# Delta net in a two-block model: the triangle built transposed, beta on its columns, and the transposed inverse taken by VectorE's transpose

## The chip, the cores and the metric

The kernel runs on one core of one Trainium2 chip. A core has TensorE (matrix products into PSUM), VectorE, ScalarE, GpSimd and SyncE (here it issues the loads of the weights), and 16 DMA engines. Times are device microseconds (us) of the whole program; the median of several executions counts.

## What is computed

Two transformer blocks on 256 tokens of width 1024, all in float32. The first block mixes the tokens in four groups of four heads (attention with forget gates, "fox"; gated delta net, "gdn"; and two gated linear attentions), the second by a short convolution and by differential attention; each ends in gated feed-forward layers. The change lies in the delta net of the first block alone. Cut to what matters:

```python
def gated_delta_chunked(q, k, v, g, beta):      # 4 heads, 4 chunks of 64 tokens, dk = dv = 64
    G = cumsum(g) within a chunk
    decay = exp(where(causal, G[r] - G[s], -inf))
    kb = k * beta[r]
    m = where(strict, (kb[r] . k[s]) * decay, 0)
    t_mat = m + I
    w = solve(t_mat, kb * exp(G)[r])
    u = solve(t_mat, v * beta[r])
    a_qk = where(causal, (q[r] . k[s]) * decay, 0)
    q_in, k_out = q * exp(G)[r], k * exp(G[-1] - G)[r]
    # over the chunks, one after the other:
    v_new = u - w @ state
    o = q_in @ state + a_qk @ v_new
    state = state * exp(G[-1]) + k_out.T @ v_new
```

The solves are done as products with the inverse of `t_mat`, a unit triangle of 64 by 64 for each of 16 pairs of head and chunk.

## The kernel before

**Weights.** All products with weights take them in blocks of 1 MB (a block is `[128, 2048]` float32), in a ring of three slots. SyncE loads block n into `raw` (`weights_in`, L462; blocks 12 and 13 in four pieces, one waiting for the other, L469 and L472) once the low part of block n-3 has been made. ScalarE rounds it to `w_hi` (`block_hi`, L1511), VectorE makes the rest `w_lo = raw - w_hi` (`block_lo`, L2263; halves of it by `half_lo`, L2693), and TensorE does three products for each pair of operands: hi x hi, lo x hi, hi x lo. `quarter(n, q)` is one fourth of block n, 12 products of 128x256; `project(n, f)` is half a block, 24 products. TensorE's instructions stand in the order in which the functions are called; so do those of the other engines. Semaphores alone tie them together.

**The delta net.** Partitions hold the 128 tokens of two chunks; a "unit" u of 8 is a pair of chunks of one head. The calls of TensorE in order, with what is written beside them by the others:

- `gdn_grams`: in PSUM bank 2 the logarithms of the decays (products with constant masks), in banks 0 and 1 the gram k.k, in banks 6 and 7 the gram k.q. ScalarE takes the exponential into `dec` (L1729).
- `gdn_turn_decay`: 16 products of 64x64 with the identity turn `dec`; ScalarE copies the result into `dec_t` (L1734, two copies of 64x512). Meanwhile VectorE makes `m_gd` = gram x beta x dec, eight instructions (L2445).
- `gdn_turn_m`, after `project(7, 1)`: 16 more such products turn `m_gd`, and ScalarE copies them into `mt_gd` (L1734 again).
- VectorE makes the first approximations of the inverse in blocks of 32x32, exact in blocks of two: `inv` from `m_gd` (`gdn_first_inverse`, L2460 to L2464) and its transpose `inv_t` from `mt_gd` (`gdn_first_turned`, L2468 to L2476), with `a_qk` = gram k.q x dec_t between them (L2453).
- Five levels follow, TensorE's loop below. In each, `gdn_cx` (16 products with 64 rows and 32 columns) multiplies `c_t`, the part of `mt_gd` that belongs to the level (VectorE, L2481), by `inv`; ScalarE copies it to `y_gd` (L1748). `gdn_xcx` then forms inv x y twice in levels 0 to 3: once as it is (bank 6) and once transposed (bank 0), 32 products of 32x32 each, and VectorE subtracts the one from `inv` and the other from `inv_t` (L2488, two instructions). Level 4 has 32 products of 32x32 only, and joins the two halves of a chunk in `inv_full`.
- `gdn_solve` multiplies `inv_full` by `vb` (v x beta) and `kbg` (k x beta x exp G), and four chunks follow.

```python
            project(7, 0)
            gdn_grams()
            gdn_turn_decay()
            project(7, 1)
            gdn_turn_m()
            project(8, 0)
            fills = [(8, 2), (8, 3), (9, 0), (9, 1), ...
            for lv in range(5):
                gdn_cx(lv)
                quarter(*fills[2 * lv])
                gdn_xcx(lv)
                quarter(*fills[2 * lv + 1])
            gdn_solve()
```

VectorE's order there is: `block_lo(7)`, `block_lo(8)`, `gdn_grams`, `gdn_first_inverse`, `gdn_first_turned`, `block_lo(9)`, and then for each level the next `c_t` (`gdn_next_block`), other work (`fox_sums` after level 0, the two halves of block 10 in levels 1 and 2, `fox_scale` in level 3, `gla_queries_and_keys` and `block_lo(11)` in level 4), and `gdn_xcx`. ScalarE's order: the exponential, the copies of the turned decays, `tokens_from(fox_v)` (L1648, results of block 7), the copies of the turned m, `block_hi(9)`, and the levels.

Lines: every product goes through one of two helpers, so that L538 (`mm`) and L587 (`add`) are lines of many places. A small float32 product shows as two records in the trace: 16 products are 32 rows.

Of the kernel before, what the change touches and what calls it, by code (L numbers as in the profile page):

```python
# [91 lines left out]
def low_base(f):  # L92
# [11 lines left out]
    "decay_by_act": ("decay", "decay_t", "mt_ready"),  # L104
    "grams": ("decay_logs", "qk_gram", "decay_turned", "m_turned"),
# [16 lines left out]
def build(nc, weights, small_in, x_in, masks_in, ident_in, channel_in, row_in, w_gk_in, p_in, table_in,  # L122
# [4 lines left out]
    with ExitStack() as ctx:  # L127
# [33 lines left out]
        gd_hi = sb("gd_hi", [P, TT, HEADS], R)  # L161
        gd_lo = sb("gd_lo", [P, TT, HEADS], R)
# [43 lines left out]
        be_g = place([P, TT, HEADS])  # L206
# [9 lines left out]
        kbg = place([P, 8, DH])  # L216
        vb = place([P, 8, DH])
# [8 lines left out]
        dec = place([P, 8, CHUNK])  # L226
        m_gd = place([P, 8, CHUNK])
# [3 lines left out]
        ngd_tri = place([P, 8, CHUNK])  # L231
        HALF = CHUNK // 2
        two_blocks = lambda v: [b.rearrange("p u n -> p (u n)").rearrange("p (u n) -> p u n", n=HALF) for b in (v[:, 0:4, :], v[:, 4:8, :])]
        inv, inv_t = two_blocks(dec)
        y_gd, pair_t_odd = two_blocks(m_gd)
# [86 lines left out]
        def block_mask(name):  # L322

            at = MASK["blocks0"] * P + ("eye", "pair_even", "pair_odd", "pair_t_even", "pair_t_odd").index(name) * HALF
            return masks.rearrange("p m n -> p (m n)")[:, at:at + HALF]
# [210 lines left out]
        def _(pe):  # L536
# [423 lines left out]
            def gdn_grams():  # L960
# [3 lines left out]
                for part in (gd_hi, gd_lo):  # L964
# [7 lines left out]
                add(o, mask("same"), ngd_tri.rearrange("p u n -> p (u n)"), False, True).then_inc(once("decay_logs")[0], 1)  # L972
# [14 lines left out]
            def gdn_turn_decay():  # L987
                pe.wait_ge(*once("decay"))
                turn_chunks(2, dec).then_inc(once("decay_turned")[0], 1)

            def gdn_turn_m():
                pe.wait_ge(sem("m_ready"), 1)
                turn_chunks(0, m_gd).then_inc(once("m_turned")[0], 1)
# [31 lines left out]
            def gdn_solve():  # L1025
                pe.wait_ge(sem("inv_t_ready"), 6)
                for t, h in ALL_UNITS:
                    m, u = u_of(t, h), t * HEADS + h
                    for c in range(2):
                        r = rows_of_chunk(c)  # L1030
                        mm(chunk_bank(2, u, c), inv_full[r, m, :], vb[r, u, :])
                for t, h in ALL_UNITS:
# [3 lines left out]
                    for c in range(2):  # L1036
                        r = rows_of_chunk(c)
                        last = mm(PS[a:a + 64, c, at:at + CHUNK], kbg[r, u, :], inv_full[r, m, :])
# [203 lines left out]
            gdn_turn_decay()  # L1242
            project(7, 1)
            gdn_turn_m()
# [249 lines left out]
        def _(act):  # L1494
# [240 lines left out]

            def gdn_turn_decay():
                act.wait_ge(*once("decay_turned"))
                chunk_copy(dec_t, 2, 0)
                chunk_copy(dec_t, 2, 1).then_inc(once("decay_t")[0], 1)

            def gdn_turn_m():
                act.wait_ge(*once("m_turned"))
                chunk_copy(mt_gd, 0, 0)
                chunk_copy(mt_gd, 0, 1).then_inc(once("mt_ready")[0], 1)
# [121 lines left out]
            gdn_turn_decay()  # L1866
            tokens_from(BLOCK_OF["fox_v"])
            gdn_turn_m()
# [370 lines left out]
        def _(dve):  # L2239
# [119 lines left out]
            def gate_parts():  # L2359
# [3 lines left out]
                mark(dve.tensor_copy(gd_hi[:, :, :], gd))  # L2363
                settle()
                mark(tt(nlf_lo[:, :, :], nlf, nlf_hi[:, :, :].bitcast(F), ALU.subtract))
                mark(tt(gd_lo[:, :, :], gd, gd_hi[:, :, :].bitcast(F), ALU.subtract))
# [15 lines left out]
            def gate_products():  # L2382
                dve.wait_ge(*once("gate_exps"))
                mark(tt(be_g, beta, e_g, ALU.mult))
# [1072 lines left out]
```

## Time and profile before

| | us |
|---|---|
| median of 3 executions | 1026.76 (1026.28 to 1027.33) |
| the profiled execution | 1027.2 |
| its span in the profile | 1025.4 |
| TensorE busy in the span | 1004.7 (98%) |
| VectorE busy | 845.2 (82%) |
| ScalarE busy | 621.6 (61%) |
| DMA, mean over the span | 172 GB/s |
| mean granted clock of TensorE | 0.997 of full speed |

The delta net's triangle and inverse take the stretch from about 56 to 96 us of the span. A row of the chain gives a start, a duration and the work; a row of the timeline merges instructions of one form that follow one another, and a bracket at its end tells how long the engine had been idle, and what ended that. PE is TensorE, DVE VectorE, ACT ScalarE, SPq SyncE's queue.

### The profile page before, as it was taken

How to read it: one execution, taken by the hardware profiler on the slowest of the kernel's cores; microseconds unless marked ns; L12 is line 12 of the kernel's file. 1: busy time of each engine (PE TensorE's matmuls, PEld its weight loads, DVE VectorE, ACT ScalarE, POOL GpSimd, SP SyncE). 2: the span in 40 equal slices, each digit the busy share in tenths (PEclk: the TensorE clock that was granted, in tenths of full speed). 3: DMA queues.
4: the chain of work that ended last, by engine and by line, in shares of the span. 5: the costliest groups of instructions: out<-in, count | busy, mean ns of one | idle time of the engine just before them, and what ended most of it. 6: DMA issues, size and time to landing. Idle time of an engine off the chain costs nothing.

```text
span 1025.4 us, 21307 instructions
## 1 busy us (share of the span) xinstructions
PE 1004.7 (98%) x8589; PEld 940.3 (92%) x8589; DVE 845.2 (82%) x1211; ACT 621.6 (61%) x856; POOL 5.8 (1%) x16
## 2 busy tenths in 40 slices
PE   6999999999999999999999999999999999999996
PEld 6998899999999999899999999999999999999985
DVE  5974797699988878878999888799775899988876
ACT  6763565566665655556665555676676666565665
POOL 0000000000000000000000000000000000000000
PEclk9999999999999999999999999999999999999998
DMA  8533223455655544566566555444534356555531
GB/s 322 180 110 106 87 81 126 161 179 204 205 197 177 199 165 165 178 234 217 185 209 208 197 194 175 154 176 151 179 124 148 126 200 205 206 196 179 198 124 42
DMA packets 26500, 176.02 MB, mean 172 GB/s; under 512 B 3229, under 2 KB 3509, under 8 KB 6080
## 3 DMA queue, kind: packets, MB, share of 16 engines
q1 hardware_dynamic: 25616, 171.31, 48.5%
q0 software_dynamic: 816, 3.73, 1.2%
q8 instruction: 52, 0.85, 0.3%
q14 instruction: 16, 0.13, 0.0%
HBM read 173.97 MB, written 2.63 MB: 172 GB/s over the span
## 4 chain that ended last, share of the span: by engine, by line
PE 92%; DVE 4%; ACT 3%; issue 1%; DMA 0%; SPq 0%; DVEq 0%; ACTq 0%
PE PS L587 79%; PE PS L538 12%; DVE w_lo L2263 1%; ACT w_hi L1511 1%; DMA raw<-weights 0%; PE PS L1416 0%; DVE arena L2660 0%; DVE h_store L2276 0%; PE PS L807 0%; PE PS L777 0%; ACT arena L1831 0%; ACT arena L1625 0%; DVE x L2780 0%; DVE arena L2915 0%; PE PS L939 0%
## 5 line engine op out<-in xcount | busy, mean ns | idle before, releaser
L587 PE MATMUL PS<-h_store,w_hi 128*128 128x256 f32 (+1 forms) x1840 | 483.4, 340 | 9.2 <-DVE w_lo L2315 8.0
L2263 DVE TENSOR_TENSOR w_lo<-raw,w_hi 128x2048 fp32r<-128x2048 f32 x156 | 357.0, 2290 | 54.8 <-ACT w_hi L1511 49.6
L587 PE MATMUL PS<-h_store,w_lo 128*128 128x256 f32 (+1 forms) x1400 | 373.2, 282 | 0.6 <-issue 0.6
L587 PEld LDWEIGHTS PS<-h_store,w_hi 128*128 128x128 f32 x1840 | 308.2, 188 | 50.1 <-DVE w_lo L2315 8.0
L1511 ACT ACTIVATE w_hi<-raw 128x2048 fp32r<-128x2048 f32 x156 | 297.9, 1910 | 76.3 <-PE PS L587 66.3
L587 PEld LDWEIGHTS PS<-h_store,w_lo 128*128 128x128 f32 (+1 forms) x1400 | 257.2, 189 | 1.0 <-issue 0.8
L587 PE MATMUL PS<-act_hi,w_hi 128*128 128x256 f32 x704 | 196.2, 280 | 0.2 <-DVE act_hi L2870 0.2
L587 PE MATMUL PS<-act_hi,w_lo 128*128 128x256 f32 x704 | 195.1, 279 | 0.0
L587 PE MATMUL PS<-act_lo,w_hi 128*128 128x256 f32 x704 | 192.0, 279 | 0.0
L587 PEld LDWEIGHTS PS<-act_hi,w_hi 128*128 128x128 f32 x704 | 132.4, 188 | 2.9 <-issue 1.3
L587 PEld LDWEIGHTS PS<-act_hi,w_lo 128*128 128x128 f32 x704 | 132.3, 188 | 0.0
L587 PEld LDWEIGHTS PS<-act_lo,w_hi 128*128 128x128 f32 x704 | 130.4, 188 | 0.0
L1946 ACT ACTIVATE arena<-PS 128x512 f32<-128x512 f32 x51 | 30.2, 592 | 87.2 <-PE PS L587 87.2
L1938 ACT ACTIVATE arena<-arena,channel 128x256 f32<-128x256 f32 x132 | 63.7, 531 | 22.4 <-DVE arena L2964 15.6
L587 PE MATMUL PS<-w_hi,h_store 128*128 128x256 f32 (+1 forms) x352 | 71.4, 307 | 0.0
L2941 DVE SCALAR_TENSOR_TENSOR arena<-arena,channel 128x254 f32<-128x254 f32 x132 | 57.9, 480 | 7.6 <-DVE arena L2937 0.3
L2937 DVE SCALAR_TENSOR_TENSOR arena<-arena,channel 128x255 f32<-128x255 f32 x132 | 57.7, 478 | 3.8 <-ACT arena L1938 3.8
L587 PEld LDWEIGHTS PS<-w_hi,h_store 128*128 128x128 f32 x352 | 54.4, 188 | 3.5 <-issue 0.4
L2962 DVE TENSOR_TENSOR arena<-PS,arena 128x512 f32<-128x512 f32 x51 | 34.9, 685 | 20.6 <-ACT arena L1946 20.6
L587 PE MATMUL PS<-w_lo,h_store 128*128 128x256 f32 (+1 forms) x176 | 45.8, 302 | 0.0
L538 PE MATMUL PS<-arena 32*32 32x32 f32 (+7 forms) x1548 | 44.9, 222 | 0.9 <-DVE arena L2660 0.4
L538 PE MATMUL PS<-h_store,w_hi 128*128 128x256 f32 x256 | 45.4, 279 | 0.0
(365 smaller groups left out, 1103.0 us busy)
## 6 DMA issues: line engine op xcount, KB each, us to landing
raw<-weights SPq DMA_DIRECT2D x155, 1024.0 KB, 4.9
raw<-weights SPq DMA_DIRECT2D x12, 256.0 KB, 3.5
arena<-masks_in SPq DMA_DIRECT2D x1, 1600.0 KB, 11.6
bias_by_key<-bias_by_distance POOLq DMA_DIRECT2D x1, 1536.0 KB, 8.7
x<-x_in SPq DMA_DIRECT2D x4, 256.0 KB, 4.6
raw<-weights SPq DMA_DIRECT2D x2, 512.0 KB, 8.4
arena<-bias_by_key POOLq DMA_DIRECT2D x1, 1024.0 KB, 7.2
result<-arena SPq DMA_DIRECT2D x4, 256.0 KB, 2.1
```

Of the source, the lines that this page charges most:

```text
L538: return pe.matmul(o, lhs, rhs, start=start, stop=stop)
L587: return pe.matmul(o, lhs, rhs, start=start, stop=stop, skip_group_check=True)
L1511: act.activation(w_hi[:, slot, :], raw[:, slot, :], ACT.Copy).then_inc(hi_ready, 1)
L1938: ins = act.activation(dst[:, c, :], src[:, c, :], ACT.Identity, scale=w, bias=b)
L1946: act.activation(low, PS[:, bank:bank + 2, TOK:512], ACT.Copy).then_inc(sem("low_copied"), 1)
L2263: tt(w_lo[:, slot, :], raw[:, slot, :], w_hi[:, slot, :].bitcast(F), ALU.subtract).then_inc(lo_ready, 1)
L2937: stt(y[:, c, 1:TOK], src[:, c, 0:TOK - 1], channel[:, bass.ds(col(1) + c, 1)], y[:, c, 1:TOK], ALU.mult, ALU.add).then_inc(ready[0], 1)
L2941: ins = stt(y[:, c, 2:TOK], src[:, c, 0:TOK - 2], channel[:, bass.ds(col(0) + c, 1)], y[:, c, 2:TOK], ALU.mult, ALU.add)
L2962: tt(z, PS[:, bank:bank + 2, 0:TOK], low, ALU.add).then_inc(sem("parts_added"), 1)
```

## The change

The triangle is built transposed at once. The constant mask and the sign of the decays' operands are exchanged (`ngd` for `gd`), so that bank 2 holds the logarithms of the transposed decays, and the exponential goes straight to `dec_t`. The gram k.k is symmetric, so gram x beta x dec_t is a transposed triangle, `mt_gd`, with beta on the other index than before. That is another triangle, M' with beta on its columns, and the identity between the two moves beta: v and k go to the solve without it (`v_gd`, `kg`), and it comes back in `ko` (through `be_rest` = beta x e_rest) and in `a_qk`, which is now eight instructions as `mt_gd` is. `gdn_turn_decay` and `gdn_turn_m` are gone on TensorE and on ScalarE. VectorE makes `inv_t` from `mt_gd` and takes `inv` by a transpose of 32x32 blocks; in levels 0 to 3 TensorE forms the product once, VectorE subtracts it from `inv` and transposes the result into `inv_t`. Core of the diff:

```diff
@@ PE @@
                 add(o.rearrange("p (u n) -> p u n", n=CHUNK), exact("eye"), units(exact("gdn_add")[:, 0:CHUNK], 8), start=True)
-                for part in (gd_hi, gd_lo):
+                for part in (ngd_hi, ngd_lo):
...
-            def turn_chunks(bank, v):
-
-                for u in range(8):
-                    for c in range(2):
-                        r = rows_of_chunk(c)
-                        last = mm(chunk_bank(bank, u, c), v[r, u, :], ident[r, r])
-                return last
...
                 if lv < 4:
-                    block_products(6, inv_t, y_gd).then_inc(sem("xcx"), 1)
-                    block_products(0, y_gd, inv_t).then_inc(sem("xcx"), 1)
+                    block_products(0, inv_t, y_gd).then_inc(sem("xcx"), 1)
                     return
...
             gdn_grams()
-            gdn_turn_decay()
             project(7, 1)
-            gdn_turn_m()
             project(8, 0)
@@ ACT @@
-                act.activation(flat(dec), PS[:, 2, :], ACT.Exp).then_inc(once("decay")[0], 1)
+                act.activation(flat(dec_t), PS[:, 2, :], ACT.Exp).then_inc(once("decay")[0], 1)
...
             gdn_grams()
-            gdn_turn_decay()
             tokens_from(BLOCK_OF["fox_v"])
-            gdn_turn_m()
             block_hi(9)
@@ DVE @@
-                mark(tt(vb, psu(2), unit(th(beta), DH), ALU.mult))
+                mark(dve.tensor_copy(v_gd, psu(2)))
...
-                mark(tt(kbg, kn, unit(th(be_g), DH), ALU.mult))
-                mark(tt(ko, kn, unit(th(e_rest), DH), ALU.mult))
+                mark(tt(kg, kn, unit(th(e_g), DH), ALU.mult))
+                mark(tt(ko, kn, unit(th(be_rest), DH), ALU.mult))
...
             def gdn_a_qk():
-                dve.wait_ge(*once("decay_t"))
+
                 dve.wait_ge(*once("qk_gram"))
-                by_bank = lambda v: v.rearrange("p (b u) n -> p b (u n)", b=2)
-                tt(by_bank(a_qk), PS[:, 6:8, 0:256], by_bank(dec_t), ALU.mult).then_inc(sem("qk_gram_read"), 1)
+                for t, h in ALL_UNITS:
+                    u = u_of(t, h)
+                    mark(stt(a_qk[:, u, :], PS[:, 6 + u // 4, (u % 4) * CHUNK:(u % 4 + 1) * CHUNK], beta[:, t, h:h + 1], dec_t[:, u, :],
+                             ALU.mult, ALU.mult))
+                settle()
 
             def gdn_first_inverse():
 
-
-                dve.wait_ge(sem("m_ready"), 1)
-                dve.wait_ge(*once("decay_turned"))
-                mark(tt(inv, m_gd[:, :, 0:HALF], units(block_mask("pair_even"), 8), ALU.mult))
-                mark(tt(inv_t, m_gd[:, :, HALF:CHUNK], units(block_mask("pair_odd"), 8), ALU.mult))
-                settle()
-                link(tt(inv, units(block_mask("eye"), 8), inv, ALU.subtract))
-                tt(inv, inv, inv_t, ALU.subtract).then_inc(sem("inv_ready"), 1)
-
-            def gdn_first_turned():
-                dve.wait_ge(*once("mt_ready"))
-                tt(c_t, mt_gd, units(packed(1), 8), ALU.mult).then_inc(sem("ct_ready"), 1)
-                gdn_a_qk()
-                dve.wait_ge(sem("qk_gram_read"), 1)
-                dve.wait_ge(sem("inv_ready"), 1)
                 mark(tt(inv_t, mt_gd[:, :, 0:HALF], units(block_mask("pair_t_even"), 8), ALU.mult))
                 mark(tt(pair_t_odd, mt_gd[:, :, HALF:CHUNK], units(block_mask("pair_t_odd"), 8), ALU.mult))
                 settle()
+                tt(c_t, mt_gd, units(packed(1), 8), ALU.mult).then_inc(sem("ct_ready"), 1)
                 link(tt(inv_t, units(block_mask("eye"), 8), inv_t, ALU.subtract))
                 tt(inv_t, inv_t, pair_t_odd, ALU.subtract).then_inc(sem("inv_t_ready"), 1)
+                dve.wait_ge(sem("inv_t_ready"), 1)
+                dve.transpose(inv, inv_t).then_inc(sem("inv_ready"), 1)
...
                 if lv < 4:
-                    for k, (x_gd, ready) in enumerate(((inv, sem("inv_ready")), (inv_t, sem("inv_t_ready")))):
-                        dve.wait_ge(sem("xcx"), 2 * lv + k + 1)
-                        tt(flat(x_gd), flat(x_gd), PS[:, 6 - 6 * k, 0:8 * HALF], ALU.subtract).then_inc(ready, 1)
+                    dve.wait_ge(sem("xcx"), lv + 1)
+                    tt(flat(inv), flat(inv), PS[:, 0, 0:8 * HALF], ALU.subtract).then_inc(sem("inv_ready"), 1)
+                    dve.wait_ge(sem("inv_ready"), lv + 2)
+                    dve.transpose(flat(inv_t), flat(inv)).then_inc(sem("inv_t_ready"), 1)
                     return
...
             gdn_grams()
             gdn_first_inverse()
-            gdn_first_turned()
+            gdn_a_qk()
             block_lo(9)
```

What TensorE has in a row around the two turns, as a piece of the difference (a count is of products, each two records of the trace; 64x64 rows on the identity are the turns; 128x256 rows belong to blocks 7 and 8):

```order
 L538 MATMUL PS<-arena 64x64 x16
 L587 MATMUL PS<-arena 128x512
 L538 MATMUL PS<-arena 64x64 x16
-L538 MATMUL PS<-ident,arena 64x64 x16
 L587 MATMUL PS<-w_hi,h_store 128x256 x16
 L587 MATMUL PS<-w_lo,h_store 128x256 x8
-L538 MATMUL PS<-ident,arena 64x64 x16
 L587 MATMUL PS<-w_hi,h_store 128x256
```

Two groups of 16 products left the queue, and the 24 products of `project(7, 1)` now follow the grams at once. In levels 0 to 3 the same engine has, each time:

```order
-L538 MATMUL PS<-arena 32x32 x64
+L538 MATMUL PS<-arena 32x32 x32
```

Half of the products of 32x32 are gone. VectorE's row from `block_lo(7)` and `block_lo(8)` to the product of level 0, before (L2445 is m_gd, L2460 to L2464 the first `inv`, L2468 `c_t`, L2453 `a_qk`, L2472 to L2476 `inv_t`, L2263 `block_lo`, L2481 the next `c_t`, L2488 the subtractions of `gdn_xcx`):

```order
59 L2263 TENSOR_TENSOR w_lo<-raw,w_hi 128x2048 x2
60 L2445 SCALAR_TENSOR_TENSOR arena<-PS,arena 128x64 x8
61 L2460 TENSOR_TENSOR arena<-arena 128x256
62 L2461 TENSOR_TENSOR arena<-arena 128x256
63 L2463 TENSOR_TENSOR arena<-arena 128x256
64 L2464 TENSOR_TENSOR arena<-arena 128x256
65 L2468 TENSOR_TENSOR arena<-arena 128x512
66 L2453 TENSOR_TENSOR arena<-PS,arena 128x512
67 L2472 TENSOR_TENSOR arena<-arena 128x256
71 L2263 TENSOR_TENSOR w_lo<-raw,w_hi 128x2048
72 L2481 TENSOR_TENSOR arena<-arena 128x512
73 L2488 TENSOR_TENSOR arena<-arena,PS 128x256 x2
```

And of the changed kernel (L2415 is `mt_gd`, L2430 and L2431 the masked pairs, L2433 `c_t`, L2434 and L2435 the subtractions, L2424 `a_qk`, L2232 `block_lo`, L2442 the next `c_t`, L2448 the one subtraction of `gdn_xcx`):

```order
60 L2415 SCALAR_TENSOR_TENSOR arena<-PS,arena 128x64 x8
61 L2430 TENSOR_TENSOR arena<-arena 128x256
62 L2431 TENSOR_TENSOR arena<-arena 128x256
63 L2433 TENSOR_TENSOR arena<-arena 128x512
64 L2434 TENSOR_TENSOR arena<-arena 128x256
65 L2435 TENSOR_TENSOR arena<-arena 128x256
66 L2437 STREAM_TRANSPOSE arena<-arena 128x256
67 L2424 SCALAR_TENSOR_TENSOR arena<-PS,arena 128x64 x8
68 L2232 TENSOR_TENSOR w_lo<-raw,w_hi 128x2048
69 L2442 TENSOR_TENSOR arena<-arena 128x512
70 L2448 TENSOR_TENSOR arena<-arena,PS 128x256
71 L2450 STREAM_TRANSPOSE arena<-arena 128x256
```

One row of first approximations is left of two, `a_qk` stands behind it and is eight instructions, and a transpose stands at the end of it and behind each level's subtraction.

## Rows read from the trace of the kernel before

**Rows 1.** The page, busy time, share of the span and instructions by engine.

```profile
PE 1004.7 (98%) x8589; PEld 940.3 (92%) x8589; DVE 845.2 (82%) x1211; ACT 621.6 (61%) x856; POOL 5.8 (1%) x16
```

**Rows 2.** Waits of TensorE over the span: us in total, times, longest.

```profile
PE PS L587 <- DVE w_lo L2315: 8.0, 1, 8.0
...
PE PS L587 <- issue: 0.6, 1, 0.6
...
PE PS L538 <- DVE arena L2660: 0.4, 1, 0.4
```

**Rows 3.** The chain that ended last, 57 to 96 us: start, us, work, records.

```profile
58.55 1.84 PE PS L538 x61
60.39 3.03 PE PS L587 x24
63.42 1.08 PE PS L538 x32
64.50 3.04 PE PS L587 x24
67.53 1.05 PE PS L538 x32
68.58 1.61 PE PS L587 x12
70.19 1.16 PE PS L538 x78
71.35 0.07 issue
71.42 0.27 PE PS L538 x9
...
75.96 1.24 PE PS L538 x83
...
83.48 0.57 issue
...
93.35 0.68 PE PS L538 x50
94.03 1.61 PE PS L587 x12
```

**Rows 4.** Timeline of VectorE, 57 to 96 us.

```profile
59.22 1.62 DVE L2445 SCALAR_TENSOR_TENSOR arena<-PS,arena 128x64 f32<-128x64 f32 x8 [0.72 <-ACT arena L1729]
60.88 0.43 DVE L2460 TENSOR_TENSOR arena<-arena 128x256 f32<-128x256 f32 x1
...
65.78 0.69 DVE L2468 TENSOR_TENSOR arena<-arena 128x512 f32<-128x512 f32 x1 [3.22 <-ACT arena L1734]
...
68.70 2.28 DVE L2263 TENSOR_TENSOR w_lo<-raw,w_hi 128x2048 fp32r<-128x2048 f32 x1
...
72.17 1.21 DVE L2584 TENSOR_REDUCE stat<-arena 128x16 f32<-128x1024 f32 x1
...
75.02 1.22 DVE L2693 TENSOR_TENSOR w_lo<-raw,w_hi 128x1024 fp32r<-128x1024 f32 x1
...
92.32 0.34 DVE L2491 TENSOR_SCALAR arena<-arena 128x256 f32<-128x256 f32 x1
94.08 0.48 DVE L2493 TENSOR_SCALAR arena<-PS,arena 128x256 f32<-128x256 f32 x1 [1.42 <-PE PS L538]
```

**Rows 5.** Timeline of ScalarE, 57 to 96 us.

```profile
60.43 1.20 ACT L1734 ACTIVATE arena<-PS 64x512 f32<-64x512 f32 x2 [1.25 <-PE PS L538]
63.46 0.84 ACT L1648 ACTIVATE arena<-PS,xn 128x256 f32<-128x256 f32 x2 [1.83 <-PE PS L587]
...
65.77 1.92 ACT L1511 ACTIVATE w_hi<-raw 128x2048 fp32r<-128x2048 f32 x1
```

**Rows 6.** Timeline of SyncE's queue, 57 to 96 us: block 12.

```profile
71.01 6.89 SPq L469 DMA_DIRECT2D raw<-weights  x3
80.77 0.31 SPq L472 DMA_DIRECT2D raw<-weights  x1
```

More of the change, by code:

```diff
@@ L103 @@
     "fox_by_dve": ("fox_sums", "fox_normed"),
-    "decay_by_act": ("decay", "decay_t", "mt_ready"),
-    "grams": ("decay_logs", "qk_gram", "decay_turned", "m_turned"),
+    "decay_by_act": ("decay",),
+    "grams": ("decay_logs", "qk_gram"),
     "bias_by_act": ("bias_rows", "lambda_exps"),
@@ L160, in build @@
         nlf_lo = sb("nlf_lo", [P, TT, HEADS], R)
-        gd_hi = sb("gd_hi", [P, TT, HEADS], R)
-        gd_lo = sb("gd_lo", [P, TT, HEADS], R)
+        ngd_hi = sb("ngd_hi", [P, TT, HEADS], R)
+        ngd_lo = sb("ngd_lo", [P, TT, HEADS], R)
         zeros_r = sb("zeros_r", [P, 512], R)
@@ L205, in build @@
         e_last = place([P, TT, 2, 2])
-        be_g = place([P, TT, HEADS])
+        be_rest = place([P, TT, HEADS])
         sq = place([P, 1024])
@@ L215, in build @@
         kn = place([P, 8, DH])
-        kbg = place([P, 8, DH])
-        vb = place([P, 8, DH])
+        kg = place([P, 8, DH])
+        v_gd = place([P, 8, DH])
         ko = place([P, 8, DH])
@@ L225, in build @@
         a_qk = place([P, 8, CHUNK])
-        dec = place([P, 8, CHUNK])
-        m_gd = place([P, 8, CHUNK])
+        inverses = place([P, 8, CHUNK])
+        y_and_pairs = place([P, 8, CHUNK])
         dec_at = arena["at"]
@@ L230, in build @@
         c_t = place([P, 8, CHUNK])
-        ngd_tri = place([P, 8, CHUNK])
+        gd_tri = place([P, 8, CHUNK])
         HALF = CHUNK // 2
         two_blocks = lambda v: [b.rearrange("p u n -> p (u n)").rearrange("p (u n) -> p u n", n=HALF) for b in (v[:, 0:4, :], v[:, 4:8, :])]
-        inv, inv_t = two_blocks(dec)
-        y_gd, pair_t_odd = two_blocks(m_gd)
+        inv, inv_t = two_blocks(inverses)
+        y_gd, pair_t_odd = two_blocks(y_and_pairs)
         inv_full = dec_t
@@ L971, in gdn_grams @@
                         mm(gram_bank(0, t, h, c), k, k)
-                add(o, mask("same"), ngd_tri.rearrange("p u n -> p (u n)"), False, True).then_inc(once("decay_logs")[0], 1)
+                add(o, mask("same"), gd_tri.rearrange("p u n -> p (u n)"), False, True).then_inc(once("decay_logs")[0], 1)
                 for c in range(2):
@@ L1030, in gdn_solve @@
                         r = rows_of_chunk(c)
-                        mm(chunk_bank(2, u, c), inv_full[r, m, :], vb[r, u, :])
+                        mm(chunk_bank(2, u, c), inv_full[r, m, :], v_gd[r, u, :])
                 for t, h in ALL_UNITS:
@@ L1037, in gdn_solve @@
                         r = rows_of_chunk(c)
-                        last = mm(PS[a:a + 64, c, at:at + CHUNK], kbg[r, u, :], inv_full[r, m, :])
+                        last = mm(PS[a:a + 64, c, at:at + CHUNK], kg[r, u, :], inv_full[r, m, :])
                 last.then_inc(sem("solved"), 1)
@@ L2362, in gate_parts @@
                 mark(dve.tensor_copy(nlf_hi[:, :, :], nlf))
-                mark(dve.tensor_copy(gd_hi[:, :, :], gd))
+                mark(dve.tensor_copy(ngd_hi[:, :, :], ngd))
                 settle()
                 mark(tt(nlf_lo[:, :, :], nlf, nlf_hi[:, :, :].bitcast(F), ALU.subtract))
-                mark(tt(gd_lo[:, :, :], gd, gd_hi[:, :, :].bitcast(F), ALU.subtract))
+                mark(tt(ngd_lo[:, :, :], ngd, ngd_hi[:, :, :].bitcast(F), ALU.subtract))
                 settle()
@@ L2383, in gate_products @@
                 dve.wait_ge(*once("gate_exps"))
-                mark(tt(be_g, beta, e_g, ALU.mult))
+                mark(tt(be_rest, beta, e_rest, ALU.mult))
                 signal(sem("gk_read"), 1)
@@ L3404, in mask_table @@
     i_blk, j_blk = r % 32, c[:, 0:32]
-    pair = (i_blk // 2 == j_blk // 2) & (j_blk < i_blk)
     pair_t = (i_blk // 2 == j_blk // 2) & (i_blk < j_blk)
-    blocks = [i_blk == j_blk, pair & (i_in < 32), pair & (i_in >= 32), pair_t & (i_in < 32), pair_t & (i_in >= 32)]
-    blocks += 3 * [i_blk < 0 * j_blk]
+    blocks = [i_blk == j_blk, pair_t & (i_in < 32), pair_t & (i_in >= 32)]
+    blocks += 5 * [i_blk < 0 * j_blk]
     for j in range(4):
@@ L3419, in mask_table @@
     one["fox_add"] = np.where(c <= r, 0.0, NEG)
-    one["gdn_add"] = np.concatenate([np.where(j_in <= i_in, 0.0, NEG), i_in <= j_in], axis=1)
+    one["gdn_add"] = np.concatenate([np.where(i_in <= j_in, 0.0, NEG), i_in <= j_in], axis=1)
     rows = [one[n] + np.zeros((P, P)) for n in MASKS]
```

28 lines of the change are left out of this document (7 added, 21 removed).

## The prediction

> **What bounds the kernel now.** I read the busy times first [rows 1]: TensorE is busy 98% of the span. The waits of TensorE come next [rows 2], to see whether the missing 2% hide a chain of other engines: apart from 8.0 us for the first weights there is one wait of 0.6 us that the profile puts down to issue, and small ones of 0.2 to 0.4 us in later places. So TensorE's queue is what sets the end, and an instruction taken out of it is worth its full time, as long as its operands come early enough for the earlier start. Third, the chain inside the delta net [rows 3]: from 58.55 us on it is nothing but TensorE, group behind group, with two pieces of issue. In this view each group of products has its own price, and those are the prices that I add up. VectorE and ScalarE idle there: VectorE waited 3.22 us for ScalarE's copy of the turned m [rows 4], ScalarE 1.25 and 1.83 us for TensorE [rows 5].
>
> **What TensorE loses.** The second turn is the group of 32 records at 63.42 us, 1.08 us. The first stands in one piece with the gram k.q, 61 records in 1.84 us; at the price of the second it takes 1.08 of them and leaves 0.76 to the gram [rows 3]. Both are gone: 2.16 us.
>
> In levels 0 to 3 the group of 64 products of 32x32 (128 records, of which the chain names some) becomes one of 32. Level 4 already has a group of 32 such products, and it took 0.68 us [rows 3]. That is the price I take for each of the four. A whole group took 1.24 us in level 1, and levels 2 and 3 repeat it: 3 x (1.24 - 0.68) = 1.68 us. Level 0 took 1.16 + 0.07 + 0.27 = 1.50 us, with an issue gap late in the group [rows 3]; 1.50 - 0.68 = 0.82 us. I count that gap as gone, since the group now ends before the place in it where the gap was. Had it stayed, the sum would be 0.26 us smaller. Sum: 2.16 + 1.68 + 0.82 = 4.66 us, some 4.7.
>
> The 0.57 us of issue at 83.48 us [rows 3] lies in a run of plain 128-wide products behind level 2. Nothing that the profile shows was awaited, and I leave it in the sum. If it is TensorE running out of fetched instructions after dense groups of tiny products, it may go, since 192 records leave in front of it in levels 0 to 2 and 64 in the turns; that is a rival below.
>
> The Trainium skill bears on this: "Runtime: NRT & Kernel Launch", section Instruction fetch mechanics, says that the sequencer fetches its instructions in blocks of 16 KiB while it executes, mostly hidden, and that branches are what breaks it. By that rule a straight piece of code would have no such gap; the trace has one of 0.57 us in straight code.
>
> **What the new order asks of VectorE.** With the turns out, TensorE is done with the grams at 58.55 + 0.76 = 59.31 us, with `project(7, 1)` 3.03 us later, 62.34, and with `project(8, 0)` at 65.38, where the products of level 0 want `inv` and `c_t` (before: 67.53) [rows 3]. VectorE's side: the eight instructions on the gram end at 59.22 + 1.62 = 60.84 as before, since the exponential comes at the same time. Two masked products of 0.43 each (overlapping a little), to 61.7; `c_t`, 0.69, to 62.4; two dependent subtractions of 0.43, to 63.2; then the transpose [rows 4]. No transpose of VectorE is in this trace. It handles 128x256 elements in one instruction, as the rows of 0.34 (one operand, SBUF) and 0.48 (PSUM) do; 0.43 us of the two-operand row lies between them, and I take that. From below it can't be under the 0.34 of the plain row by much; from above I take the longest row of VectorE there, 2.28 us [rows 4]. At 0.43 `inv` is ready at 63.7, with 1.7 us to spare; even at 2.28 the wait would be 0.2 us. So the wait that is added costs nothing up to a transpose of 2.1 us.
>
> A page has a price for it: the Trainium skill, "VectorE: DVE Perf Modes", section The three transpose paths, gives 311 ns for a 128x128 transpose in bf16 by VectorE and 390 ns by TensorE. No run here shows that figure. Scaled by columns it makes 0.4 to 0.6 us for 256 columns (an estimate from that page), and the sum would stay the same.
>
> Behind the transpose: `a_qk`, now eight instructions, 1.62 us for 0.7, and `block_lo(9)`, 2.28 us. From 63.7 they end at 65.3 and 67.6, if ScalarE has block 9 rounded. ScalarE loses four copies (1.20 us for each two), takes the results of block 7 from 62.4 on, 0.84 us, and rounds block 9 in 1.92 us, to 65.3 [rows 5]: just in time. Who waits behind `block_lo(9)`: the next `c_t`, ready at 68.3, wanted by level 1 at 70.3; TensorE for block 9, wanted at 71.4; and SyncE for block 12, whose load in four pieces (from 71.01 us on, the last issued at 80.77) now starts at 67.6 and so lands some 3 us earlier [rows 6], still before ScalarE's turn for it in level 3. So none is late.
>
> In a level TensorE now takes 1.05 + 1.61 + 0.68 + 1.61 = 4.95 us [rows 3]. After the product VectorE subtracts (0.48 at most, PSUM source), and `inv` is ready 1.1 us before the next level starts; this was so before. The transpose comes behind it, and `inv_t` is wanted only 1.61 + 1.05 + 1.61 us after the product's end. In a level VectorE gives up one subtraction for one transpose, no change. At the end the last wait, VectorE's joining of the halves (0.48) under one quarter of a block (1.61), is as before [rows 4]. The copy of v instead of a multiplication, and the moved beta, have the shapes of what they replace, far ahead of TensorE's need; costed at nothing, cover being the grams and `project(7, 0)`.
>
> So the stretch ends 4.7 us earlier, and the later stages, with TensorE as full as here, carry it to the end. The sum stands against the profiled execution, span 1025.4 in 1027.2: span 1020.7, execution 1022.5. That execution is 0.4 above the median of 1026.76, so the median comes to **1022.1 us**.
>
> **The rivals.**
> - *The issue gap goes too.* For: it stands in the densest part of TensorE's code, and is the only one over the whole span of that length on the engine; 256 records leave ahead of it. Against: it lies 0.8 us behind the small products, among plain ones. It gives 1022.1 - 0.6 = 1021.5. Only chance decides where it falls, so 37%.
> - *Fewer products, but not shorter groups.* In `gdn_cx` 32 records take 1.05 us [rows 3], more than the 64 records of level 4: the count isn't the whole price. If a group in which each product writes `PS` with a new weight costs 1.05 us here, a level saves 0.2 us, and all 2.16 + 3 x 0.19 + 0.45 = 3.2 us: 1023.6. Against it stands level 4 with the same shapes at 0.68. 8%.
> - *The transpose turns into the wait.* From 2.1 us on, `inv` is late for level 0. In the levels VectorE has, between the product of level 0 and that of level 4, four subtractions (1.9), the sums of squares (1.2), three `c_t` (2.1), two halves of block 10 (2.4), `fox_scale` (about 1.4 by the row of 1024 elements and one small one), the queries and `block_lo(11)` (3.1): 12 us and four transposes, in 4 x 4.95 = 19.8 us of TensorE. So four transposes bind from 2.0 to 2.2 us each, and each us more costs 1 + 4 = 5 us. Between 2.2 and 3.1 us the gain shrinks to nothing; that is the case of a time near 1025, 6%.
> - *Slower than before.* The same mechanism from 3.1 us a transpose on, seven times the row of 0.43: the five transposes then hold VectorE, and TensorE waits in every level. At 4 us it gives 5 x (4 - 3.1) = 4.5 us more than before, 1031. It would take a rate that no instruction of VectorE shows here. 3%.
>
> **How the numbers follow.** Forecast 44%, gap gone 37%, short saving 8%, transpose partly in the way 6%, slower 3%, 2% for others. From the first two and the third the range is 1021.5 - 0.5 to 1023.6 + 0.5, the half being the spread of the shown runs about their median: 1021.0 to 1024.1, which leaves out about 15%. A measurement tells about 0.2% (2 us) from no change: faster needs a time under 1024.7. All of the first three cases are, and half of the transposes' case: 0.91. Same 0.05, slower 0.04.
>
> **What will show it.** In the chain of the changed kernel `project(7, 1)` should start at 59.3 and level 0 at 65.4, the groups in levels 0 to 3 be 64 records in 0.68 us, and the solve start near 91 us (before 95.6). The transposes should be rows of 0.3 to 0.6 us on VectorE. TensorE's waits should show none on VectorE in that stretch; one in front of the products with `c_t` would say that the transpose or the chain to it is late. If the solve starts 4.7 us earlier and the end doesn't, a later stage is bound by something else than TensorE, which these rows deny.

## The result, and the profile after

The changed kernel takes 1021.01 us (median of 5 executions, 1020.74 to 1021.24), the one before 1026.51 in the same measurement (5 executions, 1026.28 to 1027.33); ratio 0.9944, 95% interval 0.9931 to 0.9958. It is faster by 5.5 us. The forecast was 1022.1 with a range from 1021.0: the way was right, the gain was underrated by 0.8 us (4.7 forecast, 5.5 measured), and the time stands on the very edge of the range. The profiled execution has a span of 1019.0 us (1025.4 before).

The chain of the changed kernel in the delta net, 57 to 92 us (start, us, work, records); it answers to [rows 3]:

```profile
57.66 0.91 PE PS L538 x30
58.57 5.87 PE PS L587 x48
64.44 1.05 PE PS L538 x32
65.49 1.61 PE PS L587 x12
67.11 0.68 PE PS L538 x50
67.79 1.62 PE PS L587 x12
...
77.01 0.68 PE PS L538 x50
77.69 1.61 PE PS L587 x12
79.30 1.05 PE PS L538 x32
...
89.24 1.60 PE PS L538 x62
```

The two turns are gone, so that 48 records of the projections stand in one piece; each group of 32x32 products takes 0.68 us; and the quarter at 77.69, the one behind level 2, takes 1.61 us without an issue gap. Set against the starts of before this gives the account. "Lead" is how much earlier the same work starts in this trace:

| | before | after | lead |
|---|---|---|---|
| second set of grams (k.q) | 58.55 | 57.66 | 0.89 |
| products with `c_t`, level 0 | 67.53 | 64.44 | 3.09 |
| quarter behind level 0's products | 71.68 | 67.79 | 3.89 |
| quarter behind level 2's products | 82.71 | 77.69 | 5.02 |
| products with `c_t`, level 3 | 85.15 | 79.30 | 5.85 |
| the solve | 95.65 | 89.24 | 6.41 |
| end of the span | 1025.4 | 1019.0 | 6.4 |

The turns gave 2.20 us (forecast 2.16), level 0 gave 0.80 (0.82), levels 1 and 2 together 1.13 (1.12), level 3 the remaining 0.56. That is 4.7 us, the forecast's sum. The quarter behind level 2 gave another 0.83: that is the issue gap, gone. The 0.89 us of lead at the grams lies ahead of the part that lost instructions. Over the fourteen traces of this study the first set of grams starts anywhere between 54.85 and 56.81 us, whatever the kernel, so it is spread between executions. Without it this pair of traces has 4.7 + 0.8 = 5.5 us, which is also the distance of the medians. But the interval of the ratio allows 4.3 to 7.1 us, so that the medians alone can't tell 4.7 from 5.5; the traces do.

VectorE in the same stretch (timeline, start and us first), answering to [rows 4]:

```profile
58.33 1.63 DVE L2415 SCALAR_TENSOR_TENSOR arena<-PS,arena 128x64 f32<-128x64 f32 x8 [0.70 <-ACT arena L1710]
...
62.31 0.45 DVE L2437 STREAM_TRANSPOSE arena<-arena 128x256 f32<-128x256 f32 x1
62.68 1.58 DVE L2424 SCALAR_TENSOR_TENSOR arena<-PS,arena 128x64 f32<-128x64 f32 x8
64.39 2.29 DVE L2232 TENSOR_TENSOR w_lo<-raw,w_hi 128x2048 fp32r<-128x2048 f32 x1
```

The transpose takes 0.45 us (0.43 taken) and ends at 62.76, 1.7 us before level 0 wants it (1.7 forecast). TensorE's waits show none on VectorE in this stretch.

### The profile page after: what moved, and what is told of

It reads as the page before. It is cut to its first block, busy times and chain, and to the rows that moved or that the text cites. A ratio compares the mean times of both kernels' runs of the same rounds, so it can differ in the third digit from the quotient of the medians.

```text
span 1019.0 us, 20665 instructions
## 1 busy us (share of the span) xinstructions
PE 998.6 (98%) x8269; PEld 934.9 (92%) x8269; DVE 845.2 (83%) x1215; ACT 619.2 (61%) x852; POOL 5.8 (1%) x16
## 4 chain that ended last, share of the span: by engine, by line
PE 92%; DVE 4%; ACT 3%; issue 1%; DMA 0%; SPq 0%; DVEq 0%; ACTq 0%
PE PS L587 79%; PE PS L538 12%; DVE w_lo L2232 1%; ACT w_hi L1492 1%; DMA raw<-weights 0%; PE PS L1397 0%; DVE arena L2622 0%; DVE h_store L2245 0%; PE PS L807 0%; PE PS L777 0%; ACT arena L1802 0%; ACT arena L1606 0%; DVE x L2742 0%; DVE arena L2877 0%; DVE arena L2771 0%
## 5 line engine op out<-in xcount | busy, mean ns | idle before, releaser
L2232 DVE TENSOR_TENSOR w_lo<-raw,w_hi 128x2048 fp32r<-128x2048 f32 x156 | 357.1, 2290 | 54.7 <-ACT w_hi L1492 49.4
L538 PE MATMUL PS<-arena 64*64 64x64 f32 (+7 forms) x1292 | 42.3, 227 | 0.9 <-DVE arena L2622 0.4
```

The source lines that it names most:

```text
L538: return pe.matmul(o, lhs, rhs, start=start, stop=stop)
L2232: tt(w_lo[:, slot, :], raw[:, slot, :], w_hi[:, slot, :].bitcast(F), ALU.subtract).then_inc(lo_ready, 1)
```

## The experiments

Two things were open. Where did the gap of 0.83 us go, and was its going luck? And is VectorE's slack as large as the sum said, that is, would a slower transpose have turned the change into a loss at the point named? Theory P: the gap sits at fixed places of TensorE's instruction stream, where the next piece of code has not yet come, and it comes with a dense stream of tiny products. Rivals: an accident of one execution (C), or something that follows dense work after a time, wherever that lies (D). The texts below that were put on record before the runs say F for the first form of P: TensorE runs out of fetched instructions behind dense groups of tiny products.

**The kernel before once more.** No edit.

> The kernel before, unchanged, for a second look at its trace. Theory F (the gap is TensorE running out of fetched instructions behind dense groups of tiny products): an issue gap of about 0.8 us of weight loading stands again in the same quarter of level 2, since the instructions lie at the same places. Theory C (the gap is an accident of one execution): it is missing or elsewhere. The first 56 us: in the first trace the grams began at 56.6 us, in the changed kernel's at 55.7; if that is spread of single executions, the grams start here anywhere from 55.7 to 56.6.

1026.44 us in its one execution. Its chain, in level 0 and in and behind level 2:

```profile
69.90 1.26 PE PS L538 x87
...
80.94 1.24 PE PS L538 x83
82.18 0.78 PE PS L587 x5
82.96 0.27 issue
```

The gap stands at the same instruction, smaller (0.27 us; the weight loads stood still for 0.47, for 0.78 in the first trace), and the quarter takes 2.14 us instead of 1.61, so that here it costs 0.53. The gap of level 0 isn't there at all: its group takes 1.26 us in one piece, 1.50 in the first trace. The grams start at 56.3 us, with no change of code: the start spreads. The weight loads (PEld) of the first trace, beside this:

```profile
70.12 1.14 PEld L538 LDWEIGHTS PS<-arena 32*32 32x32 f32 x120
71.42 0.15 PEld L538 LDWEIGHTS PS<-arena 32*32 32x32 f32 x8 [0.16 <-issue]
...
84.06 0.19 PEld L587 LDWEIGHTS PS<-h_store,w_lo 128*128 128x128 f32 x1 [0.78 <-issue]
```

The two gaps lie behind record 120 of level 0 and behind record 5 of the quarter behind level 2. By the calls that is 8 + 12 + 32 + 12 + 128 + 12 + 32 + 12 + 128 + 5 = 381 records.

**The second set of products put back**, result unused:

```diff
                 if lv < 4:
+                    block_products(1, y_gd, inv_t)
                     block_products(0, inv_t, y_gd).then_inc(sem("xcx"), 1)
```

> The changed kernel with the second set of 32 products of 32x32 put back in levels 0 to 3, its result unused. Sum of the prediction: 4 x 0.56 us of products, so 1021.0 + 2.3 = 1023.3. Theory F adds the gap where density brings it back: 1023.3 + 0.8 to 1.1 = 1024.3. Theory C: 1023.3, no gap in the levels.

1025.9 us (10 executions, 1024.14 to 1028.11), ratio to the kernel before 0.9995, 0.9985 to 1.0004. Half of the products that had been taken away cost nearly the whole gain. Chain of its profiled execution, and TensorE's windows (stretch, its length, busy, granted clock, DMA share and GB/s):

```profile
67.51 1.22 PE PS L538 x82
...
73.00 1.20 PE PS L538 x81
74.19 1.78 issue
75.97 0.24 PE PS L538 x2
76.21 1.68 PE PS L587 x12
77.90 1.85 PE PS L538 x32
79.75 2.86 PE PS L587 x12
82.61 1.86 PE PS L538 x128
```

```profile
74.00:76.00 2.00, 0.22 (x23) 1.00 0.51 131
76.00:78.00 2.00, 2.00 (x18) 0.90 0.35 70
78.00:80.00 2.00, 2.00 (x33) 0.50 0.21 70
```

An ordinary group takes 1.22 us (1.24 in the kernel before), so products are worth 4 x 0.54. But in level 1 a gap of 1.78 us opens two records before the end of the group, and some 1.6 us behind it the granted clock falls from 1.00 to 0.50, TensorE's lower level of 1.2 GHz. The same groups then take 1.85 instead of 1.05, 2.86 instead of 1.61 and 1.86 instead of 1.22 us. TensorE had stood for 1.8 us of otherwise unbroken work before the clock fell.

This trace is of the slowest of the ten executions, 1028.11 us. Three of them (1027.15 to 1028.11) have a mean granted clock of 0.995, the other seven (1024.14 to 1026.17, median 1025.7) 0.998, as the kernel before has; so the drop of the clock is a thing of three in ten. The seven are still 2.5 us above the 1023.2 of the products alone. A gap of the size seen here would be 1.8 of them; no trace of such an execution was kept, so that is not shown.

**The turns put back**, results unused (the two groups of 16 products stand where they stood before; ScalarE copies nothing):

```diff
             gdn_grams()
+            pe.wait_ge(*once("decay"))
+            turn_chunks(2, dec_t)
             project(7, 1)
+            pe.wait_ge(sem("ct_ready"), 1)
+            turn_chunks(0, mt_gd)
             project(8, 0)
```

> The changed kernel with the 32 products of 64x64 of the two turns put back at their places, their results unused (ScalarE doesn't copy them). The chains of before and after put the turns at 2.2 us: 1021.0 + 2.2 = 1023.2. Both theories of the gap expect none here, since the levels keep their 32 products.

1022.33 us (5 executions, 1021.74 to 1023.19), ratio 0.9963, 0.9949 to 0.9977. From the start of the first grams to the solve its chain takes 90.56 - 54.85 = 35.71 us, the changed kernel's 89.24 - 55.70 = 33.54: the turns cost 2.17 us, and no gap came. The medians differ by 1.3 us only (2.2 forecast); the start of an execution spreads by 2 us, which is enough to hide the rest, but that it did is not shown.

**Both put back.**

> Both put back: TensorE has as many instructions as before, with the new work of VectorE and ScalarE. Theory F: everything is back on TensorE, gap included: 1026.5, as before. Theory C: 1021.0 + 2.2 + 2.3 = 1025.5 with no gap.

1026.65 us (10 executions, 1026.09 to 1028.62), ratio 1.0004, 0.9994 to 1.0013: as before the change. So VectorE's and ScalarE's side of the change is worth nothing by itself; all of it is TensorE's. Its chain has the gap in the same quarter as before:

```profile
80.97 1.22 PE PS L538 x82
82.18 0.78 PE PS L587 x5
82.96 0.73 issue
83.69 1.09 PE PS L587 x7
```

Five records into the quarter behind level 2, as in [rows 3] and in the second trace of the kernel before. With the products put back and the turns away, the code in front was 64 records shorter and the gap came in level 1 instead. Accident (C) falls. Between D and P the next three decide: they move the code in the stream, and nothing else.

**The kernel before, with 16 or 32 tiny products in front**, in TensorE's idle first 8 us:

```diff
+            pe.wait_ge(*once("ones_set"))
+            for _ in range(16):        # 32 in the second
+                mm(PS[0:32, 3, 0:32], ones_r[0:32, 0:32].bitcast(F), ones_r[0:32, 0:32].bitcast(F))
             first_columns()
```

> The kernel before with 16 tiny products (32x32 on ones, result unused, 32 records) put in front of everything, in TensorE's idle first 8 us. They cost no time by themselves. Theory P (the gap sits at a fixed place of TensorE's instruction stream, a boundary at which the next piece of code has not come yet): the gap moves 32 records earlier, from the fifth group of the quarter behind level 2 into the products of level 2, near record 101 of 128. Theory D (it comes a certain time behind dense work, wherever that lies): it stays in the quarter behind level 2.

1027.47 us in its one execution. Weight loads (PEld), timeline of level 2:

```profile
81.56 0.97 PEld L538 LDWEIGHTS PS<-arena 32*32 32x32 f32 x101
83.24 0.33 PEld L538 LDWEIGHTS PS<-arena 32*32 32x32 f32 x27 [0.72 <-issue]
```

The gap moved from record 128 + 5 to record 101: by 32 records, as P said to the record. The execution has a smaller gap too, which costs 0.21 us in the products with `c_t` of level 2 (1.26 us for 1.05): the weight loads pause behind the 17th of 32, which is 15 + 12 + 101 = 128 records ahead of the large one.

> The same with 32 tiny products (64 records) in front. Theory P: the gap stands near record 69 of the 128 of level 2. Theory D: as in the trace of before, in the quarter behind level 2. For the time: 1026.5 plus or minus 1 by both, more if the gap grows beyond a us and takes the clock down as in the kernel with the products put back.

1026.69 us in its one execution. Here the place was missed: nothing near record 69 of level 2, but a gap in level 1 and one behind level 3:

```profile
74.08 1.18 PEld L538 LDWEIGHTS PS<-arena 32*32 32x32 f32 x126
...
90.01 1.01 PEld L538 LDWEIGHTS PS<-arena 64*64 64x64 f32 x32 [1.32 <-issue]
```

Counted by the calls, the two places are 382 records apart. The gap of level 1 (two records before the end of the group) and the place forecast in level 2 (record 69) are 127 apart: 2 + 12 + 32 + 12 + 69. So there are boundaries every 127 to 128 records (each comes with a weight load, so some 256 instructions), and at which of them TensorE has to stand is not fixed by the place alone; the speed at which it came there is the other part, as the dense and the thin versions show. P holds in that form. The two gaps of the trace with the products put back and with both put back are 255 records apart in the stream, which is twice that. The page's row of the instructions' own queue (packets, MB, share) fits; for the changed kernel it is

```profile
q8 instruction: 49, 0.80, 0.3%
```

16.3 KB a packet. With the turns put back (64 records and as many weight loads, 128 instructions) it counts 50, with the products (512 instructions) 51, with both, as in the kernel before (640), 52: with 256 instructions a packet these are 0.5, 2 and 2.5 packets more, where only whole ones count. The 52 don't hold the whole code, since TensorE's records and weight loads alone are 17,178; the row can be trusted for differences here, not for the total. The Trainium skill, "Runtime: NRT & Kernel Launch", section Instruction fetch mechanics, names blocks of 16 KiB or 256 instructions; the traces agree. It calls crossing one mostly hidden and finds the trouble in branches; here straight code shows gaps up to 1.8 us, so in dense streams of tiny products the measurement decides against it.

The kept traces show the arrival itself. Each packet of that queue is in them with its time. The last one before the end of each gap (us from the start of the span):

| trace | last code packet, start and duration | TensorE goes on | behind the packet's end |
|---|---|---|---|
| before, level 0 | 68.73, 1.33 | 71.42 | 1.36 |
| before, behind level 2 | 81.74, 0.94 | 84.06 | 1.38 |
| before once more | 80.64, 1.29 | 83.23 | 1.30 |
| products put back | 73.08, 1.32 | 75.97 | 1.57 |
| both put back | 81.09, 1.17 | 83.69 | 1.43 |
| before, 16 in front | 80.67, 1.22 | 83.25 | 1.36 |
| before, 32 in front, level 1 | 73.65, 0.96 | 75.98 | 1.37 |
| before, 32 in front, behind level 3 | 87.12, 1.05 | 89.80 | 1.63 |

In all eight gaps TensorE goes on 1.3 to 1.6 us behind the end of a packet of code, while the packets come 3.5 to 9 us apart there. That is what a wait for code looks like, and neither C nor D would tie the end of a gap to a packet. What decides when a packet starts isn't shown: at one and the same boundary the gap was 0.27, 0.57 and 0.73 us long in three executions. The loads of weights use the same 16 DMA engines and are a possible cause that no run separates.

**The products put back, with 32 tiny products in front**, so that the levels stand where they stood before the change:

> The changed kernel with the second set of products put back in the levels, and 32 tiny products in front, so that the levels stand at the same places of TensorE's stream as in the kernel before (the turns were 64 records). Theory P: the gap of 1.8 us in level 1 and the drop of the clock behind it are gone, and a gap of 0.5 to 0.9 us stands in the quarter behind level 2, as before: 1021.0 + 2.3 + 0.8 = 1024.1, against 1025.9 without the shift. Theory D: as without the shift, 1025.9.

1024.76 us (10 executions, 1023.20 to 1025.97), ratio 0.9983, 0.9973 to 0.9992, against 1025.9 without the shift. Its chain:

```profile
77.94 1.22 PE PS L538 x82
79.16 0.78 PE PS L587 x5
79.94 0.97 issue
80.92 1.09 PE PS L587 x7
```

The gap is back in the quarter behind level 2, the one of 1.78 us is gone, and in this trace the clock stays at 1.00 throughout the levels. In both gaps of this trace TensorE again goes on 1.3 to 1.4 us behind the end of a code packet. By the medians the kernel with 64 records more, which compute nothing, is 1.1 us faster; the intervals of the two ratios (0.9973 to 0.9992, 0.9985 to 1.0004) overlap a little, so the place of the gap in the trace carries the argument more than the time. D says neither.

**The transpose, four and eight times over.**

```diff
+                for _ in range(3):        # 7 in the second
+                    link(dve.transpose(inv, inv_t))
                 dve.transpose(inv, inv_t).then_inc(sem("inv_ready"), 1)
```

and likewise in the levels.

> The changed kernel with each transpose of VectorE done four times over (the same result), so that it takes 4 x 0.46 = 1.85 us. The prediction's slack says that up to 2.0 to 2.1 us nothing waits: 1021.0, the solve as early as before. If instead the transpose was on the edge in the levels, TensorE waits in each: above 1022.

1020.85 us (4 executions, 1020.01 to 1021.26), ratio 0.9943, 0.9928 to 0.9958. Nothing lost at 1.9 us a transpose. In the trace the last of the four in front of level 0 ends at 64.07 + 0.45 = 64.52 us and the products start at 64.77: 0.25 us are left, so that the wait would begin at 1.9 + 0.25 = 2.1 us a transpose, as forecast.

> Each transpose eight times over, 3.7 us. The prediction's rival: level 0 waits 3.7 - 2.1 = 1.6 us and the four levels behind it 1.5 us each, 1021.0 + 7.6 = 1028.6, slower than before, VectorE without idle time through the levels. If TensorE's own fill hides more than that, nearer to 1025. A wait of over a us in front of each level may take the clock down too, which would come on top.

1029.13 us (9 executions, 1028.74 to 1030.01), ratio 1.0029, 1.0019 to 1.0039: slower than before. TensorE's waits from 56 to 99 us (engine and place, released by, us, times, longest):

```profile
PE PS L538 <- DVE arena L2454: 3.3, 4, 1.2
PE PS L538 <- DVE arena L2439: 1.7, 1, 1.7
```

L2439 is the transpose in front of level 0: 1.7 us for 1.6 forecast. Behind it come 3.3 us on the transposes in the levels (6.0 forecast) and 1.8 us on VectorE's other work; in the windows of the same trace the granted clock averages 0.71 from 66 to 70 us, behind the first wait. TensorE stood 6.8 us in all where 7.6 were forecast, and it ran at the lower clock for some 3.4 us, which costs half of that, 1.7. The forecast time came out to half a us because the one made up for the other; that is luck. The rival on the other side was real all the same: its wait at level 0 was as priced, and it begins between four and eight transposes; by the 0.25 us left at four, near the place named.

**A further version.** The blocks of `c_t` outside 32x32 are zero in levels 0 to 3, so `gdn_cx` can take 32 products of 32x32 (0.68 us) for 16 with 64 rows (1.05 us):

```diff
                 for u in range(8):
+                    if lv < 4:             # lv < 2 in the later version
+                        for q, r in enumerate(QUARTERS):
+                            last = mm(block_at(2, u, r), c_t[r, u, (q % 2) * HALF:(q % 2 + 1) * HALF], inv[r, u, :])
+                        continue
                     for c in range(2):
```

> The changed kernel, and in levels 0 to 3 the products of gdn_cx taken as 32 products of 32x32 instead of 16 with 64 rows (their off-diagonal blocks are zero there). By the prices of the groups, 0.68 us for 64 records of 32x32 and 1.05 us for 32 of the larger: 4 x 0.37 = 1.5 us less than the changed kernel, 1019.5. The price of a dense stream may come against it: 128 tiny records a level again as before; if a gap of 0.8 us comes back, 1020.3, and if it is long enough to take the clock down, 1022.

1020.52 us (4 executions, 1019.93 to 1021.12), ratio 0.9939, 0.9922 to 0.9955. The groups came at 0.68 us, and a gap with them:

```profile
74.02 0.55 PE PS L538 x42
74.57 1.47 issue
76.04 0.32 PE PS L538 x15
```

Four times 0.37 us gained, 1.47 us given back in this trace. The weight loads show the place:

```profile
73.95 0.52 PEld L538 LDWEIGHTS PS<-arena 32*32 32x32 f32 x50
76.04 0.21 PEld L538 LDWEIGHTS PS<-arena 32*32 32x32 f32 x14 [1.57 <-issue]
```

By the calls the gap stands 354 records behind the start of level 0 (2 x 152 and 50 weight loads into level 2), and so does the one of 1.78 us in the kernel with the second set of products put back (184 + 32 + 12 + 126): a different kernel, the same place in the stream. TensorE goes on 1.5 us behind the end of a code packet here too. In the changed kernel the same place lies in the quarter behind level 2; counted from the start of level 0 TensorE comes there some 4 us later, when its packet (73.60 to 74.55 us) has long been in, and doesn't stand. So, half of the change:

> The products of gdn_cx as 32 products of 32x32 in levels 0 and 1 alone. If the gap of 1.47 us with all four levels so was the price of a stream of tiny instructions that outruns their loading, half of it leaves the stream slow enough: no gap, 1021.0 - 2 x 0.37 = 1020.3. If the gap stays, 1021.5.

1019.99 us (5 executions, 1019.29 to 1020.63), ratio 0.9940, 0.9926 to 0.9953, with no issue gap in the levels. From the first grams to the solve it takes 87.79 - 55.02 = 32.77 us, the changed kernel 33.54 and the kernel before 39.06 (95.65 - 56.59). In the levels of the kernel before TensorE issues 184 records in 5.5 us, here 152 in 4.6 in two levels and 120 in 4.95 in the rest, and the version with all four levels at 152 had the gap: both run alike through levels 0 and 1, and only the next 50 records, in 0.6 us there and in 2.7 us here, tell them apart. The mean over several us counts, not one group. At these rates 128 records are used up in 3.8 to 3.9 us in the dense streams and in 5.3 us in the thin one (an estimate from the counts above); the packets of code in the levels of the dense kernels come 3.4 to 6.0 us apart.

The same, and level 4 without the products that only copy:

```diff
                     for even, odd in (QUARTERS[0:2], QUARTERS[2:4]):
-                        mm(block_at(0, u, even), y_gd[odd, u, :], inv_t[odd, u, :])
-                        last = mm(block_at(0, u, odd), ident[odd, odd], inv_t[odd, u, :])
+                        last = mm(block_at(0, u, even), y_gd[odd, u, :], inv_t[odd, u, :])
```

> The same, and in level 4 the 16 products with the identity (they only copy the odd halves of the transposed inverse into PSUM) left to VectorE, which copies from SBUF instead: 32 records of 32x32 fewer, 0.3 us by the price of the group of 64 in 0.68. 1020.0, if VectorE's four instructions in place of one stay under the quarter of a block behind level 4 (1.61 us).

1019.91 us (5 executions, 1019.60 to 1021.00), ratio 0.9936, 0.9923 to 0.9950; not to be told from the one before it. Level 4's group with half of its records takes nearly as long:

```profile
87.29 0.62 PE PS L538 x32
```

0.62 us for 32 records, 0.68 for 64. The 16 products left all write the even quarters of the partitions; the 16 taken out wrote the odd ones and must have run beside them, which is argued from the two durations and not tried further. The simpler version has the gain too: 0.77 us less in the stretch than the changed kernel (0.74 forecast). By the medians it is 6.2 us under the 1026.15 of the kernel before in the same measurement, the changed kernel was 5.5 under in its own; the intervals of the two ratios overlap nearly whole, so that the gain rests on the traces.

## What the prediction had right, and the step that failed

- **What bounds the kernel**: right. What left TensorE's queue came off the end one for one: the lead of the solve (6.41) is the lead of the end (6.4). And with all of it put back, the time is that of the kernel before (ratio 1.0004, 0.9994 to 1.0013).
- **The turns**: 2.16 us forecast, 2.20 in the two traces, 2.17 with them put back alone. The split was a little off (the grams took 0.91 us and not 0.76, so the first turn 0.93), and the two projections, no longer cut apart, gave 0.20 us back.
- **The products**: 0.68 us from the row of level 4 held in all four levels, to the hundredth. The rival "fewer products, but not shorter groups" falls here; the last experiment shows it true in another place, where the products taken out had run beside others.
- **The gap of level 0**: counted as gone, and gone. But it was no fixed part of the time before: the second trace of the kernel before has none, so that 0.26 of the 4.66 us belonged to one execution.
- **The gap behind level 2**: this is the step that failed. The forecast left it in the sum ("I leave it in the sum"), gave 37% to its going, and sized it at 0.57 us, the piece in the chain. It went, and was worth 0.83 against the first trace: the quarter took 2.44 us with it and 1.61 without, and the weight loads stood still for 0.78. Against the second trace of the kernel before it was worth 0.53, with both groups put back 0.99; so its size spreads, and the half of a us that the forecast took was within that. "Only chance decides" was wrong too. The gap belongs to a stream of 184 records in 5.5 us; the change itself thinned it to 120 in 4.95. The forecast named the mechanism as a rival and gave it no weight of its own; the count that speaks for it (the gap stands 381 records, three pages of code, behind the smaller one in level 0) could have been made from the trace of before and the calls. With the gap gone the sum is 1026.76 - 4.7 - 0.8 = 1021.3, and the range would have reached below 1021.
- **VectorE's slack**: 1.7 us at level 0, measured 1.7. Binding from 2.0 to 2.2 us a transpose: no loss at 1.9, with 0.25 us left. 5 us for each us more was too much for the waits (6.8 of 7.6 us at 3.7) and left out the clock; the 1028.6 against the 1029.1 measured is near by luck.
- **The price of the transpose**: 0.43 taken, 0.45 measured for 128x256 float32.

## What to carry to other kernels

Where one engine is busy 98% of the time, price each group of its instructions by the row of a group of the same shape that already runs in the kernel; here such a sum held to a few hundredths of a us. Don't halve a row for half of the count: 32 records of level 4 took 0.62 us where 64 took 0.68. Treat an issue gap as part of the code and not as weather: count instructions between gaps, and if the counts are multiples of one number, ask whether the change makes the stream thinner or denser. And when work is moved to a second engine, work out the duration at which it would bind, since the slack, not the price, decides whether the move is safe.

## What the runs showed of the hardware

- Tiny products can outrun the loading of TensorE's own code. With 184 records in 5.5 us gaps of 0.07 to 1.8 us opened at some of the boundaries 127 to 128 records apart, and each ended 1.3 to 1.6 us behind the end of a packet of code; at 120 in 4.95 us there was none. Where they fall depends on everything in front: 32 records that do nothing moved one by 32 records, 64 others removed one of 1.78 us.
- A stand of 1.8 us in otherwise full work was followed, some 1.6 us after its end, by a granted clock of 0.50, and a wait of 1.7 us for VectorE (eight transposes) by the same about 1 us after its end; the other gaps (0.07 to 1.5 us) were not. That made the gap in one trace cost 1.78 + 0.80 + 1.25 + 0.64 = 4.5 us, more than twice its length.
- 32 products of 32x32 took 0.68 us; 16 that write only every other quarter of the partitions took 0.62.
- The same kernel's start, up to the first grams at about 56 us, spreads over 2 us between executions. The traces show two parts of it. The first product waits for the first weights, to 7.0 us in one and 8.1 us in another. And TensorE's first products follow one another at 0.21 us each, later at 0.12; the change of pace comes at 13.2 us in the first trace of the kernel before and at 11.0 in the changed kernel's, which makes 1.0 us between them (2.2 us hold ten products at 0.21, and ten at 0.12 take 1.2), less 0.1 for the later start: the 0.89 us of lead at the grams. The clock column shows 1.00 in both stretches, so it doesn't tell what the pace follows.
